# Three regroupings in a one-core block stack: the last projection by token blocks, narrow token sums in pairs, the recurrence's head norm half a round later

## The chip, the cores and the metric

The kernel runs on one core of one Trainium2 chip. The metric is the device time of one execution in microseconds (us). The kernel before was timed in three executions: 1313.74, 1315.18 and 1315.96 us, so the median is 1315.18 us. One more execution was taken with the hardware profiler; its own time is 1314.39 us, and the span that its page covers is 1312.6 us.

Five engines work side by side: PE (TensorE, matrix products into PSUM banks of 128 x 512 fp32), DVE (VectorE), ACT (ScalarE), POOL (GpSimd) and SP (SyncE, which here only issues DMAs).

## What is computed

Everything is for one sequence of 512 tokens and a model width of 1024. Two blocks run one after the other. The first has a gated MLP layer and a chunked attention layer and ends in a norm. The second takes that norm's output `x`, and has two branches:

```python
h = rms_norm(x, norm_g)
hq, hf, hi, hz, cq, ckv, kr, mz, gl = split(h @ w_in)
# branch 1: a gated linear recurrence over 8 heads of 128, then a norm per head
o = hgrn2_recurrence(silu(hq), 1 - f, hi, log(f))       # f from sigmoid(hf)
o = rms_norm_2(o, hg_norm_g) * silu(hz)                 # mean over the 128 channels of a head
# branch 2: latent attention over 8 heads -> out2 * silu(mz)
y = sigmoid(gate0) * (o @ w_proj_a) + sigmoid(gate1) * (out2 @ w_proj_b)
x = x + y @ w_out                                        # the last projection, 1024 x 1024
return rms_norm(x, final_norm_g)                         # per token, over 1024 features
```

`rms_norm` multiplies by `rsqrt(mean(x*x) + 1e-6)` and by a gain per feature. The change touches three places of this: the norm of `h` at the start of the second block (its sums over features), the norm of `o` per head, and the last projection with the residual and the final norm behind it.

## The kernel before, in words

**Layout.** Activations lie with features on the 128 partitions and the 512 tokens along the free axis: `x` is 8 tiles of 128 x 512. A product of fp32 accuracy is three products in the rounded type fp32r, high x high, low x high and high x low (`mm3`, lines 497 to 502). PE takes an fp32r product of 128 x 512 as one instruction; a plain fp32 product shows as two in the trace.

**Weights.** They come from HBM as slabs of 128 x 1024 fp32 in the order of the list `ORDER`. For each slab SP issues a DMA into one of two `raw` buffers (L474), ACT rounds it into `whi` (`cut`, L1075), POOL subtracts to get `wlo` (L490), and PE waits for that. `whi` and `wlo` have four places each, so `cut` waits until PE has used the slab four earlier. The last projection has 8 slabs (`w3`); the first four of them are put into a part of `yhi`/`ylo` that is free by then, and are loaded between the slabs of the second branch's projection (`pb`).

**A slab of PE work** is `slab(...)`: 8 blocks k, three products each, 24 in all. Its argument `between` lets other small work in behind a block k.

**The second block's first norm.** The values projection (`values(0)`, slabs `hv`) starts before the norm's factors are known. When two of its four slabs are done, `token_factors` (L743 to L749) sums the squares of every token: 8 products of one column each, plain fp32, four with `nacc` and four with `naccb`. DVE and ACT turn these into one factor per token, DVE writes them as diagonal matrices (`diag`, L1818), PE spreads them over all partitions by one plain fp32 product of 128 x 512 with a matrix of ones (L741), and DVE multiplies (`nfull`, L1825), ACT and DVE round (`hhi`, `hlo`, L1829). The next slab, `hq` of head 0, waits for `hlo` block by block.

**The recurrence.** Round r projects head r (slabs `hq`, `hf`, `hz`, and `mz` for the other branch) and runs head s = r - 1 through scores, state updates and outputs in between. The norm of head u = r - 2 is: ACT squares the output (`ho`, L1296), PE sums over the 128 channels by a plain fp32 product of 128 x 512 with ones (`hg_square`, L787, behind block 2 of slab `hq`), ACT takes Ln and Exp (L1298, L1300), DVE multiplies and rounds (`hg_finish`: L1854, L1857, L1859, L1861). On ACT `hg_root(u)` stands at the start of a round, on DVE `hg_finish(u)` too. The chain of a round that others hang on goes from the end of slab `hf` over ACT's Sigmoid and Ln (L1339, L1340) and a DVE scan to the rounded queries and keys (last of them `hqxlo`, L1935), which PE needs for `hg_diagonal` behind block 4 of the next `hq`.

**The end.** With `pb` PE alternates slabs of the second gate (`g1`). `x` had been kept in HBM and is loaded back; PE spreads the first block's norm factors by an fp32 product (L996) and DVE applies them (`normed`, L2079). The last projection runs in 16 steps of 24 products of 128 x 256 (`out_slab`): features on the partitions, tokens in two halves. DVE adds each result to `x` (L2106), ACT squares (L1513), DVE accumulates. For each half PE sums over the partitions (`out_tokens`, L1025, L1026: eight narrow products), DVE and ACT work out the factors, PE spreads them (`out_wide`, L1031) and DVE multiplies (`finished`, L2129); SP stores each 128 x 256 tile (L478). For the second half all this comes behind the last product.

## Time and profile before

| what | value |
|---|---|
| median of three executions | 1315.18 us (1313.74 to 1315.96) |
| profiled execution's own time | 1314.39 us |
| its span | 1312.6 us, 16685 instructions |
| PE busy | 1295.1 us (99%), 6531 instructions |
| DVE busy | 729.9 us (56%) |
| ACT busy | 664.4 us (51%) |
| POOL busy | 496.0 us (38%) |
| granted clock of PE | 0.996 of full speed over the span |
| HBM read, written | 123.92 MB, 10.49 MB |

The page gives for each engine the time in which it had an instruction under way. A product's end is modelled and products overlap, so what a product costs is read from the distance between two starts, not from its own duration: rows of 0.39 us for 128 x 512 follow each other every 0.23 us. A bracket at a row's end is the time in which the engine had nothing to do before it, and what ended that. Some records of products are missing from the trace.

### The profile page before, as it was taken

The page shows a single profiled execution, that of the slowest core. Times are in us where ns is not written, and L with a number is a line of the kernel's source. Part 1 is how long each engine was busy: PE and PEld are TensorE (multiplying, and loading weights), DVE is VectorE, ACT ScalarE, POOL GpSimd, SP SyncE. Part 2 cuts the span into 40 slices and gives each one's busy share as a digit, 9 for nine tenths or more (in the row PEclk, how much of TensorE's full clock was granted, in tenths as well). Part 3 has the DMA queues.
Part 4 walks back from the last instruction along what each step waited for, and adds up shares of the span by engine and source line. Part 5 has one row for each costly group of instructions (what it writes and reads, how often), then busy time and mean ns, then how long its engine had stood idle before and what let it go on. Part 6 is the DMA issues. An engine that isn't in the chain of part 4 may idle for free.

```text
span 1312.6 us, 16685 instructions
## 1 busy us (share of the span) xinstructions
PE 1295.1 (99%) x6531; PEld 1087.0 (83%) x6531; DVE 729.9 (56%) x1305; ACT 664.4 (51%) x999; POOL 496.0 (38%) x207
## 2 busy tenths in 40 slices
PE   9999999999999999999999999999999999999997
PEld 7888888888887788888878888888878888888897
DVE  5556556561146465555875577666645556643554
ACT  5535544443234666675546566666445545552321
POOL 4443444434444323221536343333333333334620
PEclk9999999999999999999999999999999999999999
DMA  5732322334333322322343322222223222335411
GB/s 183 262 118 90 103 84 86 100 94 150 98 112 95 96 80 94 96 63 64 95 148 111 93 65 80 70 77 65 80 81 99 78 80 82 90 105 174 154 41 65
DMA packets 43455, 131.31 MB, mean 100 GB/s; under 512 B 7088, under 2 KB 11888, under 8 KB 42864
## 3 DMA queue, kind: packets, MB, share of 16 engines
q1 hardware_dynamic: 38144, 116.41, 28.9%
q10 hardware_dynamic: 5232, 13.83, 3.0%
q8 instruction: 52, 0.85, 0.3%
q14 instruction: 27, 0.22, 0.1%
HBM read 123.92 MB, written 10.49 MB: 102 GB/s over the span
## 4 chain that ended last, share of the span: by engine, by line
PE 80%; DVE 11%; ACT 6%; issue 2%; POOL 0%; DMA 0%; DVEq 0%; SPq 0%; ACTq 0%
PE banks L500 24%; PE banks L502 24%; PE banks L501 24%; PE banks L681 2%; DVE hd L1897 1%; PE banks L673 1%; PE banks L662 1%; DVE naccb L1802 1%; DVE ylo L1699 1%; PE banks L596 1%; ACT L1340 1%; ACT L1339 1%; PE banks L906 1%; PE banks L787 1%; DVE hb L1894 1%
## 5 line engine op out<-in xcount | busy, mean ns | idle before, releaser
L490 POOL TENSOR_TENSOR wlo<-raw,whi 128x1024 fp32r<-128x1024 f32 (+2 forms) x198 | 485.0, 2452 | 738.4 <-ACT whi L1075 738.2
L500 PE MATMUL banks<-hhi,whi 128*128 128x512 f32 x752 | 304.5, 405 | 2.2 <-DVE hlo L1829 1.2
L502 PE MATMUL banks<-hlo,whi 128*128 128x512 f32 x752 | 294.1, 391 | 0.0
L501 PE MATMUL banks<-hhi,wlo 128*128 128x512 f32 x752 | 294.0, 391 | 0.0
L1075 ACT ACTIVATE whi<-raw 128x1024 fp32r<-128x1024 f32 (+2 forms) x198 | 205.4, 1038 | 170.9 <-PE banks L502 104.5
L500 PE MATMUL banks<-yhi,whi 128*128 128x512 f32 x448 | 176.8, 395 | 0.2 <-DVE ylo L1699 0.2
L502 PE MATMUL banks<-ylo,whi 128*128 128x512 f32 x448 | 174.7, 390 | 0.0
L501 PE MATMUL banks<-yhi,wlo 128*128 128x512 f32 x448 | 174.5, 389 | 0.0
L500 PEld LDWEIGHTS banks<-hhi,whi 128*128 128x128 f32 x752 | 141.9, 189 | 32.1 <-issue 2.9
L502 PEld LDWEIGHTS banks<-hlo,whi 128*128 128x128 f32 x752 | 141.5, 188 | 30.4
L501 PEld LDWEIGHTS banks<-hhi,wlo 128*128 128x128 f32 x752 | 142.1, 189 | 26.9 <-issue 2.2
L500 PEld LDWEIGHTS banks<-yhi,whi 128*128 128x128 f32 x448 | 84.1, 188 | 21.0 <-issue 3.2
L502 PEld LDWEIGHTS banks<-ylo,whi 128*128 128x128 f32 x448 | 84.1, 188 | 18.0
L501 PEld LDWEIGHTS banks<-yhi,wlo 128*128 128x128 f32 x448 | 84.2, 188 | 17.3 <-issue 0.2
L500 PE MATMUL banks<-whi,yhi 128*128 128x512 f32 x224 | 88.6, 396 | 0.7 <-DVE ylo L1555 0.6
L502 PE MATMUL banks<-wlo,yhi 128*128 128x512 f32 x224 | 87.2, 389 | 0.0
L501 PE MATMUL banks<-whi,ylo 128*128 128x512 f32 x224 | 87.2, 389 | 0.0
L500 PEld LDWEIGHTS banks<-whi,yhi 128*128 128x128 f32 x224 | 42.0, 188 | 11.4 <-issue 1.2
L501 PEld LDWEIGHTS banks<-whi,ylo 128*128 128x128 f32 x224 | 42.1, 188 | 8.9 <-issue 0.5
L502 PEld LDWEIGHTS banks<-wlo,yhi 128*128 128x128 f32 x224 | 42.0, 188 | 8.7
L1212 ACT ACTIVATE sc<-sc,sm 128x128 f32<-128x128 f32 (+1 forms) x64 | 35.1, 550 | 27.5 <-DVE sm L1757 27.5
L1655 DVE TENSOR_TENSOR mt<-mt,sz 128x512 f32<-128x512 f32 x16 | 26.3, 1642 | 37.8 <-ACT sz L1155 37.5
(383 smaller groups left out, 2205.9 us busy)
## 6 DMA issues: line engine op xcount, KB each, us to landing
raw<-w SPq DMA_DIRECT2D x193, 512.0 KB, 3.6
rel_tab<-relx ACTq DMA_DIRECT2D x1, 4096.0 KB, 21.0
tab<-rel_tab SPq DMA_DIRECT2D x16, 224.0 KB, 3.5
x<-xt ACTq DMA_DIRECT2D x1, 2048.0 KB, 9.3
x_kept<-x ACTq DMA_DIRECT2D x1, 2048.0 KB, 7.5
parts_kept<-mcg SPq DMA_DIRECT2D x8, 256.0 KB, 4.4
mgt<-parts_kept SPq DMA_DIRECT2D x8, 256.0 KB, 4.0
x<-x_kept ACTq DMA_DIRECT2D x1, 2048.0 KB, 8.0
```

The costliest lines, as they stand in the source:

```text
L490: nc.gpsimd.tensor_tensor(lo[:, begin:width], raw[:, n % 2, begin:width], f32(hi[:, begin:width]), ALU.subtract).then_inc(lo_done, 1)
L500: nc.tensor.matmul(dst, a[0], b[0], start=first, stop=False)
L501: nc.tensor.matmul(dst, a[1], b[0], start=False, stop=False)
L502: return nc.tensor.matmul(dst, a[0], b[1], start=False, stop=last)
L596: nc.tensor.matmul(mixes[q][:, t, :, :], vhi[:, t, cols], wts[:, q, :, :], start=True, stop=False)
L662: done = nc.tensor.matmul(banks[:, c:c + QW[t]], a[rows, t * P:(t + 1) * P], b[rows, 0:QW[t]], start=first, stop=last)
L673: last = nc.tensor.transpose(banks[:, c:c + P], sc[:, q, of:of + P], ident)
L681: last = nc.tensor.matmul(bank[AO[i][q]][:, k * P:S], av[q][:, i, k, :], p[:, q, AK[q][k]:AK[q][k] + KW[k]], start=k == 0 and p is phi, st ...
L787: nc.tensor.matmul(bank[6], ones, ho[:, 0, :], start=True, stop=True).then_inc(hoP.did("ms"), 1)
L1075: nc.scalar.activation(parts(slab)[0][:, begin:width], raw[:, n % 2, begin:width], ACT.Copy).then_inc(hi_done, 1)
L1212: e = nc.scalar.activation(row, row, ACT.Exp, bias=sm[:, q, 1, t:t + 1], accum_out=sm[:, q, 2, t:t + 1])
L1655: V.tensor_tensor(mt[:, q, :], mt[:, q, :], sz[:, q, :], ALU.mult).then_inc(uzV.did(f"y{q}"), 1)
```

## The change

**1. Token sums in pairs.** The eight narrow products no longer stand in one block between the second and third slab of `values(0)`. Each pair (one of `nacc`, one of `naccb`) follows one group of the third slab: behind blocks t = 1, 2, 3 of k = 4 and t = 0 of k = 5. The spreading product moves from behind the third slab to behind k = 6, t = 0 in the fourth.

**2. The head's norm half a round later.** ACT rounds the square into `hsqhi` and DVE the rest into `hsqlo`, both fp32r. PE sums them by two fp32r products with ones (`hones`), now behind block 1 of slab `hf` instead of block 2 of `hq`. ACT's Ln and Exp move from the round's start to behind the query's Silu; DVE's `hg_finish` moves behind the third state and ahead of `hstlo`. The sum goes to bank 2 (bank 6 for the last head), so slab `hz` waits for the Ln that reads it.

**3. The last projection by token blocks.** The product is turned: 8 groups (g, t), g a half of the features and t one of four token blocks, each with `mgh`/`mgl` stationary and four slabs' columns moving, 24 products of 128 x 512. Each group has a PSUM bank of its own. For that the residual `x` is turned too: PE transposes it in 32 products of 128 x 128 (`residual_turned`, half of them behind `pb` 2, half behind `pb` 4), and `normed` reads them with a token's factor as a scalar per partition and the gain from `fin1`, a row of 1024 spread over the partitions by DMA. ACT squares each result and sums along the free axis in the same instruction; the final factor is then a number per partition, with no product on PE. DVE finishes the upper feature half, ACT the lower, and each stores its own (SP and ACT queue, 128 x 512 each). The last four `w3` slabs come in another order, so that they lie in the ring's places in order.

```diff
-    return order + [("w3", n) for n in range(KT)]
+    return order + [("w3", n) for n in (0, 1, 2, 3, 6, 7, 4, 5)]
...
+W3B = (2, 3, 4, 5, 6, 7, 0, 1)
+GROUPS = [(g, t) for g in range(2) for t in range(TT)]
...
@@ PE, values(half) @@
-                    if half == 0 and j == 2:
-                        token_factors()
...
                             done = mm3(bank[4 + t], a, b, k == 0, k == KT - 1)
+                            if half == 0 and 1 <= TT * (k - 4) + t <= TT:
+                                token_sums(TT * (k - 4) + t - 1)
+                            if half == 0 and k == KT - 2 and t == 0:
+                                pe.wait_ge(n2V.sem, n2V.at("diag"))
+                                nc.tensor.matmul(bank[3], ones, diag[:, 0, :], start=True,
+                                                 stop=True).then_inc(n2P.did("wide"), 1)
...
@@ PE, the recurrence @@
             def hg_square(u):
-                pe.wait_ge(hoA.sem, hoA.at("sq", u))
-                pe.wait_ge(htV.sem, htV.at("far", u))
-                nc.tensor.matmul(bank[6], ones, ho[:, 0, :], start=True, stop=True).then_inc(hoP.did("ms"), 1)
+                pe.wait_ge(hoV.sem, hoV.at("sqlo", u))
+                if u < HH - 1:
+                    pe.wait_ge(htA.sem, htA.at("z", u + 1))
+                else:
+                    pe.wait_ge(htV.sem, htV.at("far", u))
+                nc.tensor.matmul(sum_bank(u), hones[:, :], hsqhi[:, :], start=True, stop=False)
+                nc.tensor.matmul(sum_bank(u), hones[:, :], hsqlo[:, :], start=False, stop=True).then_inc(hoP.did("ms"), 1)
 
             def hg_scores(r, k):
                 s, u = r - 1, r - 2
-                if k == 2 and u >= 0:
-                    hg_square(u)
...
             def hg_updates(s, k):
+                if k == 1 and s >= 1:
+                    hg_square(s - 1)
...
+                if r >= 2:
+                    pe.wait_ge(hoA.sem, hoA.at("ln", r - 2))
                 slab("hz", r, bank[2], h, between=outputs)
...
@@ PE, the end @@
+            def residual_turned(g):
+                if g == 0:
+                    pe.wait_ge(ld_x3, 16)
+                    pe.wait_ge(mtV.sem, mtV.all())
+                else:
+                    pe.wait_ge(x3V.sem, x3V.at(f"x{TT - 1}"))
+                for t in range(TT):
+                    for k in range(TT):
+                        last = nc.tensor.transpose(bank[4 + t][:, k * P:(k + 1) * P], x[:, TT * g + k, t * P:(t + 1) * P], ident)
+                last.then_inc(x3P.did(f"turn{g}"), 1)
...
+            def out_group(at, ks=range(KT)):
+                g, t = GROUPS[at]
+                pe.wait_ge(lo_done, max(LD["w3", TT * g + c] for c in range(TT)) + 1)
+                rows = slice(t * P, (t + 1) * P)
                 for k in ks:
                     if at == 0:
                         pe.wait_ge(mgV.sem, mgV.at("lo", k))
+                    last = mm3(bank[W3B[at]], (mgh[:, k, rows], mgl[:, k, rows]),
+                               [u[:, :, k * P:(k + 1) * P] for u in w3_parts[g]], k == 0, k == KT - 1)
+                if KT - 1 in ks:
+                    last.then_inc(w3P.did(f"g{at}"), 1)
...
@@ ACT @@
+            def hg_square(u):
                 if u >= 1:
                     act.wait_ge(hoV.sem, hoV.at("ylo", u - 1))
                 act.wait_ge(htP.sem, htP.at("o", u))
                 nc.scalar.activation(ho[:, 0, :], bank[3], ACT.Square).then_inc(hoA.did("sq"), 1)
+                act.wait_ge(hoA.sem, hoA.at("sq", u))
+                act.wait_ge(hpV.sem, hpV.at("k", min(u + 1, HH - 1)))
+                nc.scalar.activation(hsqhi[:, :], ho[:, 0, :], ACT.Copy).then_inc(hoA.did("sqhi"), 1)
+
+            def hg_root(u):
                 act.wait_ge(hoP.sem, hoP.at("ms", u))
...
                     hg_query(r)
+                    if u >= 0:
+                        hg_root(u)
                     cut()
                     hg_forget(r)
...
             act.dma_start(x[:, :, :], xs).then_inc(ld_x3, 16)
+            act.dma_start(fin1[:, :], fins[0, :].partition_broadcast(P)).then_inc(ld_fin, 16)
+            act.dma_start(fin2[:, :], fins[1, :].partition_broadcast(P)).then_inc(ld_fin, 16)
...
+            for at, (g, t) in enumerate(GROUPS):
+                if at < 2:
+                    cut()
+                    cut()
+                act.wait_ge(w3V.sem, w3V.at(f"x{at}"))
+                nc.scalar.activation(mgt[:, at % 2, :], x[:, at, :], ACT.Square,
+                                     accum_out=rt3[:, 0, g, t:t + 1]).then_inc(w3A.did(f"sq{at}"), 1)
+                if g == 1:
+                    act.wait_ge(w3V.sem, w3V.at(f"inv{t}"))
+                    nc.scalar.activation(rt1[:, 2, t:t + 1], rt1[:, 1, t:t + 1], ACT.Sqrt).then_inc(w3A.did(f"root{t}"), 1)
+                    act.wait_ge(w3A.sem, w3A.at(f"root{t}"))
+                    nc.scalar.activation(x[:, t, :], x[:, t, :], ACT.Copy,
+                                         scale=rt1[:, 2, t:t + 1]).then_inc(w3A.did(f"low{t}"), 1)
+                    act.wait_ge(w3A.sem, w3A.at(f"low{t}"))
+                    act.dma_start(out[t, :, 0:S], x[:, t, :]).then_inc(st_out, 16)
...
@@ DVE @@
+            def hg_square(u):
+                dve.wait_ge(hoA.sem, hoA.at("sqhi", u))
+                V.tensor_tensor(hsqlo[:, :], ho[:, 0, :], f32(hsqhi[:, :]), ALU.subtract).then_inc(hoV.did("sqlo"), 1)
...
+                if s >= 1:
+                    hg_finish(s - 1)
                 dve.wait_ge(htA.sem, htA.at("sthi", s))
                 V.tensor_tensor(hsts[1][:, :, :], hst[:, :, :], f32(hsts[0][:, :, :]),
                                 ALU.subtract).then_inc(htV.did("stlo"), 1)
...
                 if r >= 2:
-                    hg_finish(r - 2)
+                    hg_square(r - 2)
...
+            for at, (g, t) in enumerate(GROUPS):
+                dve.wait_ge(w3P.sem, w3P.at(f"g{at}"))
+                V.tensor_tensor(x[:, at, :], x[:, at, :], bank[W3B[at]], ALU.add).then_inc(w3V.did(f"x{at}"), 1)
+                if 1 <= at <= TT:
+                    gained(at - 1)
+                if at == TT:
+                    V.tensor_scalar(rt3[:, 1, 0, :], rt3[:, 0, 0, :], 1.0 / D, EPS, ALU.mult, ALU.add).then_inc(w3V.did("part"), 1)
+                    dve.wait_ge(w3V.sem, w3V.at("part"))
+                if g == 1:
+                    one = slice(t, t + 1)
+                    dve.wait_ge(w3A.sem, w3A.at(f"sq{at}"))
+                    V.scalar_tensor_tensor(rt1[:, 0, one], rt3[:, 0, 1, one], 1.0 / D, rt3[:, 1, 0, one], ALU.mult,
+                                           ALU.add).then_inc(w3V.did(f"mean{t}"), 1)
+                    dve.wait_ge(w3V.sem, w3V.at(f"mean{t}"))
+                    V.reciprocal(rt1[:, 1, one], rt1[:, 0, one]).then_inc(w3V.did(f"inv{t}"), 1)
+                    dve.wait_ge(w3A.sem, w3A.at(f"root{t}"))
+                    V.scalar_tensor_tensor(x[:, at, :], x[:, at, :], rt1[:, 2, one], fin2[:, S:D], ALU.mult,
+                                           ALU.mult).then_inc(w3V.did(f"high{t}"), 1)
```

How the instructions stand now, at three places. Line numbers of the changed kernel are its own.

PE in a middle round of the recurrence, before: the fp32 sum (L787) stands behind block 2 of slab `hq`, ahead of the key transposes (L758).

```order
L500 MATMUL banks<-hhi,whi 128x512
L501 MATMUL banks<-hhi,wlo 128x512
L502 MATMUL banks<-hlo,whi 128x512
L787 MATMUL banks<-ho,cst 128x512
L500 MATMUL banks<-hhi,whi 128x512
L501 MATMUL banks<-hhi,wlo 128x512
L502 MATMUL banks<-hlo,whi 128x512
L758 MATMUL banks<-cst,hkb 128x128 x3
```

After: two fp32r products (`hsqhi`, `hsqlo` with `hones`) behind block 1 of slab `hf`.

```order
L505 MATMUL banks<-hhi,whi 128x512
L506 MATMUL banks<-hhi,wlo 128x512
L507 MATMUL banks<-hlo,whi 128x512
L796 MATMUL banks<-hsqhi,hones 128x512
L797 MATMUL banks<-hsqlo,hones 128x512
L505 MATMUL banks<-hhi,whi 128x512
L506 MATMUL banks<-hhi,wlo 128x512
L507 MATMUL banks<-hlo,whi 128x512
```

The one instruction of plain fp32 is gone from `hq`, and two rounded ones stand a slab later, ahead of the state updates.

ACT in the same round, before: from the rounding of the scores (L1323) over the query's Silu (L1333) and a slab's rounding (L1075) to Sigmoid and Ln (L1339, L1342) and the rounding of the states (L1327).

```order
L1323 ACTIVATE hshi<-hs 128x512
L1333 ACTIVATE hq<-banks 128x512
L1075 ACTIVATE whi<-raw 128x1024
L1339 ACT_TABLE_LOAD
L1339 ACTIVATE he<-banks 128x512
L1340 ACT_TABLE_LOAD
L1342 ACTIVATE hf<-he,lb 128x512
L1327 ACTIVATE hsthi<-hst 128x384
L1075 ACTIVATE whi<-raw 128x1024
```

After: Ln and Exp of the norm (L1298, L1300) stand between the Silu and the slab's rounding (L1070 now), each with a table load of its own.

```order
L1323 ACTIVATE hshi<-hs 128x512
L1333 ACTIVATE hq<-banks 128x512
L1298 ACT_TABLE_LOAD
L1298 ACTIVATE ho<-banks,cst 128x512
L1300 ACT_TABLE_LOAD
L1300 ACTIVATE ho<-ho 128x512
L1070 ACTIVATE whi<-raw 128x1024
L1339 ACT_TABLE_LOAD
L1339 ACTIVATE he<-banks 128x512
L1340 ACT_TABLE_LOAD
L1342 ACTIVATE hf<-he,lb 128x512
L1327 ACTIVATE hsthi<-hst 128x384
```

Two activations moved in here and brought two table loads, where there were none with them before.

DVE at the very end, before: the last residual sum (L2106), the second half's factors (L2121 to L2125), and eight tiles to finish (L2129).

```order
L2106 TENSOR_TENSOR x<-x,banks 128x256
L2121 TENSOR_SCALAR rt<-banks 128x2
L2123 RECIPROCAL rt<-rt 128x2
L2125 TENSOR_TENSOR nr<-cst,rt 128x256
L2129 SCALAR_TENSOR_TENSOR x<-x,vec,banks 128x256 x8
```

After: the last residual sum (L2118), one token block's factor (L2127, L2130), one tile to finish (L2132), behind the finishing of the block before.

```order
L2130 RECIPROCAL rt<-rt 128x1
L2132 SCALAR_TENSOR_TENSOR x<-x,rt,fin 128x512
L2118 TENSOR_TENSOR x<-x,banks 128x512
L2127 SCALAR_TENSOR_TENSOR rt<-rt 128x1
L2130 RECIPROCAL rt<-rt 128x1
L2132 SCALAR_TENSOR_TENSOR x<-x,rt,fin 128x512
```

Of the eight finishing multiplications of 128 x 256 behind the last product, one of 128 x 512 is left on DVE (one of the same size is now ACT's), and the diagonal matrix that PE had to spread is gone.

## Rows read from the trace of the kernel before

**Rows 1.** Timeline of PE, one recurrence round: start, duration, engine, line, operation, tiles.

```profile
870.04 0.39 PE L502 MATMUL banks<-hlo,whi 128*128 128x512 f32 x1
870.58 1.12 PE L787 MATMUL banks<-ho,cst 128*128 128x512 f32 x2 [0.15 <-ACT ho L1296]
...
871.78 0.40 PE L501 MATMUL banks<-hhi,wlo 128*128 128x512 f32 x1
...
873.28 0.22 PE L500 MATMUL banks<-hqxhi,hkhi 128*128 128x128 f32 x1
```

**Rows 2.** Timeline of ACT, middle of the same round.

```profile
851.46 0.58 ACT L1333 ACTIVATE hq<-banks 128x512 f32<-128x512 f32 x1
855.17 1.06 ACT L1075 ACTIVATE whi<-raw 128x1024 fp32r<-128x1024 f32 x1 [3.13 <-PE banks L502]
856.25 1.28 ACT L1339 ACT_TABLE_LOAD   x1
```

**Rows 3.** Timeline of ACT, the norm of the last head.

```profile
963.62 0.69 ACT L1298 ACTIVATE ho<-banks,cst 128x512 f32<-128x512 f32 x1 [4.42 <-PE banks L787]
...
965.62 0.63 ACT L1300 ACTIVATE ho<-ho 128x512 f32<-128x512 f32 x1
```

**Rows 4.** Timeline of DVE, the round of rows 1 and 2.

```profile
845.02 2.50 DVE L1859 CAST yhi<-ho 128x512 fp32r<-128x512 f32 x1
...
860.72 0.56 DVE L1886 TENSOR_TENSOR hstlo<-hst,hsthi 128x384 fp32r<-128x384 f32 x1 [5.97 <-ACT hsthi L1327]
...
870.60 1.09 DVE L1935 TENSOR_TENSOR hqxlo<-hqx,hqxhi 128x896 fp32r<-128x896 f32 x1
```

**Rows 5.** Timeline of PE, the token sums in the values projection.

```profile
667.40 1.02 PE L747 MATMUL banks<-cst,nacc 128*128 128x1 f32 x8 [0.34 <-DVE naccb L1802]
...
669.49 0.40 PE L501 MATMUL banks<-whi,ylo 128*128 128x512 f32 x1
...
684.58 0.50 PE L500 MATMUL banks<-hhi,whi 128*128 128x512 f32 x1 [0.64 <-DVE hlo L1829]
```

**Rows 6.** Timeline of DVE, the factors written as diagonals.

```profile
670.81 0.69 DVE L1818 TENSOR_TENSOR diag<-cst,rt 128x512 f32<-128x512 f32 x1 [0.27 <-ACT rt L1282]
```

**Rows 7.** Timeline of PE, ten transposes of 128 x 128 in the attention.

```profile
1040.83 1.25 PE L906 MATMUL banks<-cst,msc 128*128 128x128 f32 x10
...
1042.15 0.40 PE L501 MATMUL banks<-hhi,wlo 128*128 128x512 f32 x1
```

**Rows 8.** Timeline of PE, the slab behind the fourth slab of `pb`.

```profile
1222.50 0.47 PE L500 MATMUL banks<-hhi,whi 128*128 128x512 f32 x1 [0.31 <-POOL wlo L490]
```

**Rows 9.** Timeline of PE: last `pb` slab, last projection's first and last product.

```profile
1249.78 0.39 PE L500 MATMUL banks<-yhi,whi 128*128 128x512 f32 x1
...
1255.22 0.28 PE L500 MATMUL banks<-mgh,yhi 128*128 128x256 f32 x1
...
1302.31 0.28 PE L502 MATMUL banks<-mgl,whi 128*128 128x256 f32 x1
```

**Rows 10.** Line 590, moving operand in two strided runs: ns min/median/max, starts.

```profile
L590 PE MATMUL banks<-wts,rones x16: 282/282/386, 113.9 to 275.9; 128*128 128x256 f32 x16
```

**Rows 11.** Timeline of DVE, behind the last product.

```profile
1302.62 0.42 DVE L2106 TENSOR_TENSOR x<-x,banks 128x256 f32<-128x256 f32 x1 [0.73 <-PE banks L502]
1304.70 0.16 DVE L2121 TENSOR_SCALAR rt<-banks 128x2 f32<-128x2 f32 x1 [1.66 <-PE banks L1026]
...
1305.33 0.42 DVE L2125 TENSOR_TENSOR nr<-cst,rt 128x256 f32<-128x256 f32 x1 [0.27 <-ACT rt L1517]
1306.55 3.22 DVE L2129 SCALAR_TENSOR_TENSOR x<-x,vec,banks 128x256 f32<-128x256 f32 x8 [0.79 <-PE banks L1031]
```

**Rows 12.** Timeline of ACT: what an accumulating activation adds.

```profile
1172.72 0.19 ACT L1488 ACTIVATION_READ_ACCUMULATOR msc<-msc,msm 128x1 f32 x1
```

**Rows 13.** DMA issues: tiles, queue, count, size of one, us to landing.

```profile
raw<-w SPq DMA_DIRECT2D x193, 512.0 KB, 3.6
...
out<-x SPq DMA_DIRECT2D x16, 128.0 KB, 1.8
```

234 lines of the change are left out of this document (76 added, 158 removed).

## The prediction, made before the changed kernel was run

> **What bounds the kernel now.** I read the page's table of busy times first: PE has something under way in 99% of the span, no other engine in more than 56%. So a microsecond of PE's work or of PE's waiting is a microsecond of the kernel, work on DVE, ACT or POOL counts only where PE waits for it, and DMA only at the very end. Then I read PE's own timeline at the places that the diff touches. Distances between starts are the price list. A 128 x 512 product in fp32r takes 0.227 us: the last `pb` slab has 24 of them in 5.44 us [rows 9]. The reader is to see four things. In a recurrence round PE first waits for ACT's square and then spends long on the plain fp32 sum [rows 1]. In the values projection it waits for DVE and then does narrow sums [rows 5]. The last projection takes from 1255.22 to 1302.31 us [rows 9]. Behind its last product 10.3 us pass until the span's end at 1312.6, with DVE doing eight multiplications at the end of them [rows 11].
>
> **Part 2, the head's norm.** From 870.04 to 871.78 there are 1.74 us in which two ordinary distances (0.45) would stand, so wait and fp32 sum together cost 1.29: 0.31 of wait (0.54 between the first two starts, less 0.23) and 0.97 for the sum (870.58 to 871.78, less 0.23) [rows 1]. Two fp32r products cost 0.45. Seven heads stand in this position, one every 29.6 us, all with the same distances: 7 x (1.29 - 0.45) = 5.9 us. The last head's sum has no wait before it: 0.97 - 0.45 = 0.5. Together -6.3 to -6.4; I take **-6.3**.
>
> That counts the wait as gone, so what is late next? On the clock of before: PE's first diagonal product stood at 873.28 [rows 1], and without the 1.29 us it stands at 872.0. It needs `hqxlo`, ready at 870.60 + 1.09 = 871.69 [rows 4]. 0.3 us are left, less the hand-off. I take that as no wait; if it fails it costs what is missing, seven times.
>
> In the round's middle Ln and Exp are inserted on ACT with a table load each, ahead of the slab rounding at 855.17, which starts when slab `hf` ends, and the Sigmoid behind it, from which the round's chain starts [rows 2]. The slab now holds the sum, so it ends 0.45 later, at 855.6. If the query's Silu ends where it did, at 851.46 + 0.58 = 852.04, the insert ends at 852.04 + 1.28 + 0.69 + 1.28 + 0.63 = 855.9 [rows 2, 3], 0.3 late. But the Silu stands behind a rounding that waits for DVE's masks, and DVE's masks stood behind `hg_finish`, with a cast that alone takes 2.50 [rows 4]; with that moved away I estimate the Silu 0.7 earlier and the insert's end at 855.2. So the cover is ACT's idle 3.13 us before 855.17 [rows 2], and I take nothing for it. Between the two ends, 0 and 0.3 us a round, lies up to 2 us.
>
> The new waits: `hg_square` on PE waits for DVE's rest of the square (`hsqlo`), made more than half a round before; queued behind it is all of slab `hf`. Slab `hz` waits for the Ln, which ends near 853.9 at the latest, when `hf` is not yet through. On DVE `hg_finish` now starts near 855.3 and takes the cast's 2.50 and three operations of 128 x 512 at about 0.7 each (estimated from 1.09 for 128 x 896 [rows 4]), 4.6 in all, to 859.9. Behind it is `hstlo`, which waits for ACT until 860.72, and 0.45 later now [rows 4]. It is in time by over 1 us, in the 5.97 us that DVE stood idle. The rounding of the square and the earlier slab rounding on ACT fall where nobody waits.
>
> **Part 1, the pairs.** The block of sums runs from 667.40 to 669.26 (669.49 less 0.23), after a wait of 0.34 [rows 5]: 1.86 us for eight. Pairs between long products I price the same, 0.45 each. PE saves the wait, since the first pair comes 1.4 us later than the block did. But it is not PE that this stage ends with: slab `hq` waits for `hlo` at 684.58 and PE stands for 0.64 us there [rows 5], and that chain starts at the spreading product. Before, that came 24 products behind the sums: 669.26 + 5.44 = 674.7. Now it comes behind nine groups of three (6.1 us) and four pairs (1.8 us), counted from 667.06: 675.0. The factors are ready: they took until 670.81 + 0.69 = 671.50 [rows 6], 2.24 behind the sums, and the last pair now ends at 667.06 + 3.4 + 1.8 = 672.3, which gives 674.5. So what PE saves it gives back as a longer wait for `hlo`: **+0.2**, between -0.5 (wait gone, nothing given back) and +0.5.
>
> **Part 3, the stage with `pb`.** Off goes one fp32 spreading product: -0.97, by the sum in [rows 1]. On come 32 transposes of 128 x 128; ten take 1042.15 - 0.23 - 1040.83 = 1.09 us [rows 7], so 32 take +3.5. POOL's late slab costs PE 0.31 at 1222.50, about 0.4 with the restart [rows 8]; PE will now come there 0.97 earlier and 1.75 (sixteen transposes) later, 0.8 late in sum, while POOL's slabs hang on loads and not on PE. That wait goes: -0.4. Sum **+2.1**. The gains `fin1` and `fin2` put 1 MB more on the DMA engines. At 3.6 us for 512 KB [rows 13] that is up to 7 us of transfer. It is issued right behind the load of `x`, when all four places of the ring are full, and is needed some 25 us later, so I take 0 of a possible 0 to 3.
>
> **The last projection.** Before: 1255.22 to 1302.31 + 0.12 = 47.2 us, with 384 products, one set of token sums and one spreading product inside [rows 9]. After: 192 x 0.227 = 43.5. **-3.7.** The moving operand now lies in four runs of 128. Were each run to cost like a product of its own, 0.11 [rows 7], it would be 4 x 0.11 - 0.23 = 0.21 more per product, 40 us in all. Line 590 streams 256 columns in two such runs in 282 ns [rows 10], the same as the 0.28 of a contiguous 256 [rows 9], so I take nothing.
>
> **Behind the last product.** Before: 10.3 us from its start. After, from the start of the last one: DVE begins 0.42 later (0.31 for 256 columns [rows 11], 0.11 more of streaming), adds 512 columns (0.73 with the hand-off), ACT squares (0.63 as the Exp [rows 3]) and reads the accumulator (0.19 [rows 12]), mean, reciprocal and root take 1305.33 - 1304.70 = 0.63 [rows 11], and DVE's last multiplication 0.75, while ACT does its half beside it. That is 3.4. Then two stores of 256 KB. One of 128 KB lands in 1.8, a load of 512 KB in 3.6 [rows 13]; I take 3.0, since both run together, and 0.1 for hand-offs. 6.5 against 10.3: **-3.8**, with ends -5.0 and -3.2.
>
> **Sum.** -6.3 + 0.2 + 2.1 - 3.7 - 3.8 = -11.5 us. From the profiled execution's own 1314.4 that gives 1302.9; the median of the three runs stands 0.8 above that execution, which would give 1303.7. I forecast 1303.3.
>
> **Rivals.**
> A, slower. The insert on ACT is not covered. It decides from the point where Exp ends more than 0.3 us behind the end of `hf`: from there the Sigmoid, the scan and `hqxlo` come late by the same amount, PE waits at the diagonal, and every microsecond counts seven times. It turns the forecast into a loss from 1.9 us of lateness. If a table load held the engine as long again as its 1.28, the insert would end at 857.8, 2.2 behind 855.6: 7 x 1.9 = 13.3, and the time is 1314.4 - 11.5 + 13.3 = 1316.2. Against it: between Ln's end at 964.31 and Exp's start at 965.62 there are 1.31 us, just one load [rows 3]. For it: three loads in a row is a pattern with no idle time between them that the trace does not show. The Trainium skill, page "ScalarE: Activation LUTs", section "What ACT_TABLE_LOAD costs", states a load of about 1283 ns and a drain of about 1380 ns on top for each change of set. By that rule two more changes a round would come to 2.8 us more than I count, and as an estimate the time would be near 1317; the trace has the load at that length and no drain beside it, so the trace decides. 5%.
> B. The chain takes over in the rounds. The 0.3 us of room at the diagonal products is used up by hand-offs and by ACT's insert, and PE waits 0.3 to 0.4 there each round: 7 x 0.35 = 2.5 less gain, 1305.8. The narrow room speaks for it; DVE's lighter start of a round speaks against. 15%.
> C. The end gives less: the two final stores are slow (3.6 or more instead of 3.0), or the 1 MB delays a slab while `pb` runs and PE waits 2 us more. 1305.8. The wait at 1222.50 [rows 8] shows that slabs are tight there. 13%.
> D. The stage does not do what it says: a strided moving operand streams slower than rows 10 shows for two runs. Even a tenth of the bound above is 4 us: 1307. 3%.
> The forecast itself has 64%, with its own range from 1301 to 1305.
>
> **How the numbers follow.** A measurement of this kernel tells no change from about 0.2% (2.6 us). A, 5%, is slower, or close to no change if milder. B, C and D are faster, as the forecast is; two of them together still are. I set faster 0.92, same 0.03, slower 0.05. The range takes in the low ends (-0.5 in part 1, -5.0 at the end: 1301) and B and C together at the high end: 1300.5 to 1308.
>
> **What would show it.** Right: no product of `ho` in PE's timeline, `hsqhi` and `hsqlo` 0.23 apart, and round period 28.8 instead of 29.6; ACT's slab rounding in the middle still begins when PE ends `hf`; transposes in two blocks of 1.75 us; groups of 5.44 us; the span ends 6 to 7 us behind the last product. Wrong: ACT goes from Exp straight into the rounding with PE's `hf` long done; a wait of PE for `hqxlo`; a wait for POOL between `pb` 2 and `pb` 5; products of 128 x 512 in the last projection more than 0.24 apart.

## The result

The changed kernel takes 1306.56 us (median of five executions, 1304.92 to 1310.23), the one before 1315.18. The ratio is 0.9934, with a 95% interval of 0.9924 to 0.9944: 8.6 us by the medians. The two profiled executions differ by 9.5 us (1314.39 and 1304.92; spans 1312.6 and 1303.1). The forecast was 1303.3 with a range of 1300.5 to 1308, so the time lies inside, 3.3 us above the point.

Busy times first, from the page of the kernel after:

```profile
span 1303.1 us, 16288 instructions
...
PE 1286.9 (99%) x6349; PEld 1077.0 (83%) x6349; DVE 728.6 (56%) x1286; ACT 690.1 (53%) x1027; POOL 498.4 (38%) x207
```

PE still bounds everything. Its busy time has fallen by 8.2 us. The other 1.3 us are a balance of idle time: behind the last product PE stands 2.2 us less, in the middle rounds 1.0 less, in the last round 1.6 more.

The two timelines of PE can be laid side by side, since the same products stand in both. What the starts of the same product differ by, after less before, at the marks between the stages (the last column is the step from one mark to the next):

| mark (a product of PE) | before | after | step |
|---|---|---|---|
| first product with `hkb`, end of the first norm's stage | 724.07 | 724.28 | +0.21 |
| first product with `hkthi`, last round | 940.03 | 934.77 | -5.47 |
| first product with `hqbhi`, last round | 952.58 | 949.08 | +1.76 |
| sums of `dsq`, downward projection | 975.77 | 971.93 | -0.34 |
| spreading of `ddiag` | 984.77 | 979.57 | -1.36 |
| last product with `msc`, end of attention | 1174.49 | 1169.40 | +0.11 |
| first product of the last projection | 1255.22 | 1252.26 | +2.13 |
| last product of the last projection | 1302.31 | 1296.65 | -2.70 |
| end of the span | 1312.6 | 1303.1 | -3.84 |

The sum is -9.5.

**The middle rounds went as forecast.** PE's timeline after, in the sixth round; it answers to [rows 1]. Columns: start and duration in us, engine, line, result and operands, shape, count.

```profile
868.04 0.49 PE L765 MATMUL banks<-cst,hkb 128*128 128x128 f32 x3
...
869.07 0.22 PE L505 MATMUL banks<-hqxhi,hkhi 128*128 128x128 f32 x1
...
875.23 0.39 PE L796 MATMUL banks<-hsqhi,hones 128*128 128x512 f32 x1
875.46 0.39 PE L797 MATMUL banks<-hsqlo,hones 128*128 128x512 f32 x1
875.69 0.39 PE L505 MATMUL banks<-hhi,whi 128*128 128x512 f32 x1
```

The two rounded products cost 0.23 each, and no row carries a bracket: no wait for the square, none for `hqxlo` at the diagonal products (869.07). ACT's timeline of the same kernel one round earlier, to be held against [rows 2, 3]; the bracket at the end is idle time before the instruction and what ended it:

```profile
847.16 0.58 ACT L1333 ACTIVATE hq<-banks 128x512 f32<-128x512 f32 x1
847.76 1.28 ACT L1298 ACT_TABLE_LOAD   x1
849.06 0.69 ACT L1298 ACTIVATE ho<-banks,cst 128x512 f32<-128x512 f32 x1
849.76 1.28 ACT L1300 ACT_TABLE_LOAD   x1
851.06 0.63 ACT L1300 ACTIVATE ho<-ho 128x512 f32<-128x512 f32 x1
852.26 1.06 ACT L1070 ACTIVATE whi<-raw 128x1024 fp32r<-128x1024 f32 x1 [0.56 <-PE banks L507]
```

The insert ends at 851.69, and the slab rounding still waits 0.56 us for PE: it is covered, with that much room. The period of a round is 28.85 us (before 29.62).

**The last round did not.** The same insert there, on ACT, DVE, POOL and PE:

```profile
938.80 1.06 ACT L1070 ACTIVATE whi<-raw 128x1024 fp32r<-128x1024 f32 x1 [5.00 <-PE banks L507]
939.87 1.28 ACT L1298 ACT_TABLE_LOAD   x1
941.17 0.69 ACT L1298 ACTIVATE ho<-banks,cst 128x512 f32<-128x512 f32 x1
...
943.83 0.75 DVE L1863 SCALAR_TENSOR_TENSOR ho<-banks,vec,ho 128x512 f32<-128x512 f32 x1 [5.46 <-ACT ho L1300]
...
945.38 2.63 POOL L495 TENSOR_TENSOR wlo<-raw,whi 128x1024 fp32r<-128x1024 f32 x1 [3.04 <-ACT whi L1070]
945.80 2.75 DVE L1870 TENSOR_TENSOR ylo<-ho,yhi 128x512 fp32r<-128x512 f32 x1
948.48 0.55 DVE L1897 TENSOR_TENSOR hstlo<-hst,hsthi 128x384 fp32r<-128x384 f32 x1
949.08 0.33 PE L505 MATMUL banks<-hqbhi,hsthi 128*128 128x128 f32 x1 [1.59 <-DVE hstlo L1897]
```

PE waits 1.59 us for `hstlo`. Two things stand in its way. ACT idles 5.00 us at a slab rounding that stands ahead of Ln, so DVE's finish of head 6 starts only at 943.83. And DVE's `ylo`, 0.69 us where nothing else runs, takes 2.75 beside POOL's slab.

**The end.** PE's blocks of transposes and the last projection, and DVE's and ACT's work behind the last product; they answer to [rows 7, 9, 11, 12]:

```profile
1205.17 1.91 PE L1010 MATMUL banks<-cst,x 128*128 128x128 f32 x16
...
1228.71 1.91 PE L1010 MATMUL banks<-cst,x 128*128 128x128 f32 x16
...
1252.26 0.40 PE L505 MATMUL banks<-yhi,mgh 128*128 128x512 f32 x1
...
1296.65 0.40 PE L507 MATMUL banks<-wlo,mgh 128*128 128x512 f32 x1
1297.08 0.69 DVE L2118 TENSOR_TENSOR x<-x,banks 128x512 f32<-128x512 f32 x1 [2.73 <-PE banks L507]
...
1299.19 0.75 DVE L2132 SCALAR_TENSOR_TENSOR x<-x,rt,fin 128x512 f32<-128x512 f32 x1 [0.27 <-ACT rt L1524]
```

From 1252.26 to 1296.65 there are 191 distances of 0.2324 us, not 0.227. Behind the last product 3.3 us of work and 3.1 us of store follow, 6.45 in all.

**A stretch of half clock** in the profiled run of before makes the step of -1.36 at `ddiag`. Windows at the same place of the program, three of before and then one of after (the window ahead of it has 1.00 as well); the column ahead of the last two is PE's granted clock:

```profile
972.00:976.00 4.00, 2.71 (x13) 1.93 (x13) 3.90 (x4) 1.25 (x2) 2.60 (x1) 1.00 0.45 133
976.00:980.00 4.00, 4.00 (x24) 3.53 (x24) 3.81 (x7) 0.34 (x2) 2.37 (x1) 0.86 0.45 141
980.00:984.00 4.00, 4.00 (x14) 3.17 (x13) 2.30 (x5) 3.95 (x5) 0.86 (x1) 0.71 0.16 56
```

```profile
972.00:976.00 4.00, 4.00 (x26) 3.62 (x27) 3.84 (x6) 0.40 (x1) 2.37 (x1) 1.00 0.49 139
```

In both PE has just waited 1.3 us for DVE's sums of `dsq`. Before, the clock then fell from 2.4 to 1.2 GHz for a while: 0.14 x 4 + 0.29 x 4 = 1.7 us lost. After, it did not, in that execution. In others it seems to: the kernel after has mean clocks of 0.995 to 0.999, and its execution of 0.995 is the slow one, 1310.23. Between the marks the stretch cost less than 1.7, namely the 1.36 of the table. So 1.4 of the 9.5 us between the two profiled executions is chance, and the medians' 8.6 is the fairer number.

### The profile page after: what moved, and what is told of

Read it like the earlier page. It is cut to its first block, busy times and chain, and to the rows that moved or that the text cites. A ratio compares the mean times of both kernels' runs of the same rounds, so it can differ in the third digit from the quotient of the medians.

```text
span 1303.1 us, 16288 instructions
## 1 busy us (share of the span) xinstructions
PE 1286.9 (99%) x6349; PEld 1077.0 (83%) x6349; DVE 728.6 (56%) x1286; ACT 690.1 (53%) x1027; POOL 498.4 (38%) x207
## 4 chain that ended last, share of the span: by engine, by line
PE 92%; DVE 5%; ACT 2%; issue 1%; DMA 0%; SPq 0%; DVEq 0%; ACTq 0%
PE banks L505 28%; PE banks L507 28%; PE banks L506 28%; PE banks L686 2%; PE banks L678 1%; PE banks L667 1%; DVE ylo L1702 1%; PE banks L601 1%; PE banks L919 1%; DVE nfull L1698 1%; DVE hlo L1832 0%; DVE nfull L1828 0%; DMA raw<-w 0%; PE banks L951 0%; PE banks L950 0%
## 5 line engine op out<-in xcount | busy, mean ns | idle before, releaser
L505 PE MATMUL banks<-hhi,whi 128*128 128x512 f32 x752 | 300.3, 399 | 2.5 <-DVE hlo L1832 1.9
L1070 ACT ACTIVATE whi<-raw 128x1024 fp32r<-128x1024 f32 (+2 forms) x198 | 205.3, 1038 | 155.7 <-PE banks L507 98.2
```

The source lines that it names most:

```text
L505: nc.tensor.matmul(dst, a[0], b[0], start=first, stop=False)
L1070: nc.scalar.activation(parts(slab)[0][:, begin:width], raw[:, n % 2, begin:width], ACT.Copy).then_inc(hi_done, 1)
```

## The experiments

In each the marks above were read again. The front part of the program starts up to 0.7 us later or earlier from one execution to the next, so distances between marks are compared, and times of whole executions only with their ratio.

### The head's norm alone

The kernel before, with only this part of the change (its main lines, against the kernel before):

```diff
@@ PE, hg_updates @@
+                if k == 1 and s >= 1:
+                    hg_square(s - 1)
...
@@ ACT @@
                     hg_query(r)
+                    if u >= 0:
+                        hg_root(u)
...
@@ DVE, hg_stage @@
+                if s >= 1:
+                    hg_finish(s - 1)
```

> The kernel before with only the head's norm changed (two rounded products behind block 1 of slab hf, Ln and Exp in the round's middle). Theory: the terms are separate and add. Seven rounds get 0.78 us shorter each (-5.5), the last head's sum gives -0.3, and in the last round PE waits for hstlo, +1.8, because DVE does the whole finish of head 6 ahead of it. Sum -4.0: about 1311.2 by median, round period 28.85 us, one wait of PE of 1.6 us near 949 us + 0 in the last round. Rival: the wait for hstlo comes only with the other parts of the change (other phase of POOL and DVE); then the sum is -5.8, 1309.4, and PE has no wait for hstlo.

1311.16 us (ten executions, 1309.74 to 1313.99), ratio to before 0.9967 (0.9958 to 0.9976). The last round's `hkthi` stands at 934.59, 5.44 us earlier than before; then comes:

```profile
948.90 0.33 PE L508 MATMUL banks<-hqbhi,hsthi 128*128 128x128 f32 x1 [1.59 <-DVE hstlo L1917]
```

The wait for `hstlo` belongs to this part and to no other. The rival is out. The -4.0 us expected was measured as -4.0 at the sums of `dsq` (971.75 against 975.77), and as -4.6 by the medians.

### Contiguous moving operand

```diff
-                               [u[:, :, k * P:(k + 1) * P] for u in w3_parts[g]], k == 0, k == KT - 1)
+                               [u[:, k // 2, (k % 2) * S:(k % 2 + 1) * S] for u in w3_parts[g]], k == 0, k == KT - 1)
...
-            "pb": _feature_slabs(i["w_proj_b_2"][0]), "w3": _feature_slabs(i["w_out_2"][0])}
+            "pb": _feature_slabs(i["w_proj_b_2"][0]), "w3": _token_slabs(i["w_out_2"][0])}
```

> The changed kernel, but the last projection's weights lie in the slabs by pairs of blocks k, so that the moving operand of each product is 512 contiguous columns instead of four runs of 128. Nothing else is different. Theory: the runs cost. Distance between products in the last projection falls from 0.2324 to 0.2267 us, 192 x 0.0057 = 1.1 us, first to last product 43.3 us, and the kernel is 1.1 us faster than the changed one (about 1305.5). Rival: the longer distance comes from something else in that stretch (the stationary operand, DVE and ACT in the same memory, the banks); then the distance stays 0.232 and the time is that of the changed kernel (1306.6).

The theory fell. From first to last product it is 1298.08 - 1253.68 = 44.40 us, as in the changed kernel (44.39). Four runs of 128 cost nothing. The time, 1308.13 us (six executions, 1305.10 to 1310.38), is no different from the changed kernel's within their spreads.

### The last round's Ln and Exp first

```diff
                 else:
-                    cut()
                     hg_root(u)
                     hg_states(s)
                     cut()
+                    cut()
```

> The changed kernel, but in the last round ACT does head 6's Ln and Exp and the rounding of the states ahead of the slab rounding for which it waits 5 us. Theory: PE's wait of 1.6 us for hstlo (at 949.08 us) is caused by Ln and Exp standing behind that slab rounding; with them at about 934 instead of 940 us DVE has finished head 6 by about 942 and hstlo is there by 943, 4 us ahead of PE. The wait and its restart go: -1.8 us, about 1304.8 by median. Rival 1: ACT's slab rounding then comes late and PE waits for a slab instead, gain 0 to 0.5. Rival 2: what PE saves it gives back at the downward projection's wait of 1.3 us (970 to 972 us), which then grows to 3 us; gain 0.

1304.86 us (1304.70 to 1306.58), ratio 0.9922 (0.9910 to 0.9934). DVE's timeline:

```profile
938.82 0.75 DVE L1863 SCALAR_TENSOR_TENSOR ho<-banks,vec,ho 128x512 f32<-128x512 f32 x1
...
940.79 2.77 DVE L1870 TENSOR_TENSOR ylo<-ho,yhi 128x512 fp32r<-128x512 f32 x1
943.49 0.55 DVE L1897 TENSOR_TENSOR hstlo<-hst,hsthi 128x384 fp32r<-128x384 f32 x1
```

The finish starts 5 us earlier, `hstlo` is there at 944.04, and PE's wait is gone. From `hkthi` to the sums of `dsq` it is 35.34 us instead of 37.16: -1.82, as expected, with the wait at `dsq` unchanged at 1.30. No slab came late there; PE waited 0.39 us once for POOL in the `pb` stage.

### The narrow sums in a block, the spreading product earlier

```diff
-                            if half == 0 and 1 <= TT * (k - 4) + t <= TT:
-                                token_sums(TT * (k - 4) + t - 1)
-                            if half == 0 and k == KT - 2 and t == 0:
+                            if half == 0 and k == 4 and t == 1:
+                                for tt in range(TT):
+                                    token_sums(tt)
+                            if half == 0 and k == 5 and t == 1:
```

> The changed kernel, but all eight narrow sums stand in one block where the first pair stands (behind block t = 1 of k = 4), and the spreading product stands 12 products later (behind t = 1 of k = 5). Theory: what ends this stage is the chain spreading product, nfull, hlo, not PE. The block costs PE what four pairs cost (0 to 0.1 us difference), the spreading product starts near 672.7 us instead of 674.9, and PE's three waits for hlo (1.31, 0.28 and 0.30 us) go: -1.5 to -2.0 us, about 1304.8 by median. Rival 1: pairs between long products are cheaper than a block; then the block costs more (+0.5 or more) and the gain is 1.0 to 1.4. Rival 2: hlo is late because DVE and ACT, not the spreading product, are behind; the waits stay, gain 0. In both, PE may wait for the diagonal at the new place if the factors take over 2.5 us.

1304.96 us (1303.33 to 1308.10), ratio 0.9924 (0.9912 to 0.9936). Changed kernel first, then the experiment:

```profile
674.94 1.02 PE L743 MATMUL banks<-diag,cst 128*128 128x512 f32 x2
...
684.78 0.50 PE L505 MATMUL banks<-hhi,whi 128*128 128x512 f32 x1 [1.31 <-DVE hlo L1832]
...
686.03 0.50 PE L505 MATMUL banks<-hhi,whi 128*128 128x512 f32 x1 [0.28 <-DVE hlo L1832]
```

```profile
673.25 1.02 PE L744 MATMUL banks<-diag,cst 128*128 128x512 f32 x2
...
685.63 0.50 PE L505 MATMUL banks<-hhi,whi 128*128 128x512 f32 x1 [0.30 <-DVE hlo L1833]
```

From the first sums with `naccb` to the first product with `hkb` it is 53.74 us instead of 55.81: -2.07. The stage ends with the chain that starts at the spreading product. In a block or in pairs, the sums cost PE the same (1.79 and 1.81 us); what counts is where the spreading product stands.

One link of that chain is longer than it need be. In the changed kernel, DVE and POOL ahead of PE's wait of 1.31 us:

```profile
681.76 2.41 POOL L495 TENSOR_TENSOR wlo<-raw,whi 128x1024 fp32r<-128x1024 f32 x1 [4.66 <-ACT whi L1070]
682.50 2.22 DVE L1832 TENSOR_TENSOR hlo<-nfull,hhi 128x512 fp32r<-128x512 f32 x1
```

The other `hlo` take 0.69 us. This one takes 2.22 and ends 0.55 us behind POOL's slab; at 0.69 it would have ended at 683.19, ahead of PE's own arrival near 683.3. The experiment leaves that stretch in place (2.25 us) and only brings it forward, out of PE's way. No run moved POOL's slab here.

### One table load instead of two

```diff
             def hg_root(u):
+                act.preload_act_table_set("natural_log_exp_and_others")
                 act.wait_ge(hoP.sem, hoP.at("ms", u))
```

> The changed kernel, but ahead of Ln the set of ACT's tables is loaded that has both Ln and Exp, so that one load of 1.28 us stands in the insert instead of two. Theory: the insert ends 0.56 us ahead of the slab rounding that waits for PE (852.26 us), so it is covered, and a shorter one brings nothing: round period stays 28.85 us, the rounding's idle time grows from 0.56 to 1.84 us, time 1306 (as the changed kernel, within 1 us). In the last round Exp ends 1.3 us earlier, with it hstlo, and PE's wait there shrinks from 1.6 to 0.3 us: -1.3 us once. Rival: the insert is part of the round's chain; then each of six rounds gets up to 0.4 us shorter, -2.5 us more.

1303.41 us (1302.53 to 1304.45), ratio 0.9908 (0.9891 to 0.9924). The rounds keep their period of 28.85 us: the insert was covered, and the rival is out. But the last part gains more than the expected 1.3: from `hkthi` to the sums of `dsq` it is 34.08 us instead of 37.16. The wait for `hstlo` goes completely (-1.8) and not only by 1.3: DVE reaches `ylo` at 945.02, ahead of POOL's slab at 945.87, and `ylo` takes 0.69 us instead of 2.75. The wait at `dsq` goes too (-1.3), because the last head's Ln and Exp also stand on the way to DVE's sums of `dsq`. That second place the expectation had missed.

### One load more

```diff
                 nc.scalar.activation(ho[:, 1, :], ho[:, 1, :], ACT.Exp, scale=-0.5).then_inc(hoA.did("root"), 1)
+                for n in range(1):
+                    act.preload_act_table_set(("natural_log_exp_and_others", "exp_and_others")[n % 2])
```

> The changed kernel with one more load of a table (1.28 us) behind Exp in every head's insert. Theory: the insert has 0.56 us of room until the slab rounding, and hqxlo behind it 0.28 us until PE's diagonal products (ready at 868.77, wanted at 869.05). So 1.28 us more makes PE wait 0.44 us for hqxlo in each of the six middle rounds, +2.6 us, and another 1.3 us in the last round (hstlo later): about 1310.5, round period 29.3. Rival 1 (the forecast's rival A taken as a rule: every microsecond of ACT's insert counts in full): +1.28 x 6 + 1.3 = +9.0, 1315.6. Rival 2 (more cover than counted): no wait at the diagonal, only the last round's +1.3: 1307.9.

1308.49 us (1307.31 to 1309.07), ratio 0.9943 (0.9928 to 0.9957). PE's wait, as expected within 0.1 us:

```profile
872.03 0.33 PE L505 MATMUL banks<-hqxhi,hkhi 128*128 128x128 f32 x1 [0.34 <-DVE hqxlo L1948]
```

Six rounds have it, and their period is 29.43 us: +0.58 each, of which 0.34 is wait and the rest restart and products that then stand further apart. ACT behind Exp:

```profile
853.52 0.63 ACT L1300 ACTIVATE ho<-ho 128x512 f32<-128x512 f32 x1
854.17 1.28 ACT L1302 ACT_TABLE_LOAD   x1
855.47 1.06 ACT L1070 ACTIVATE whi<-raw 128x1024 fp32r<-128x1024 f32 x1
```

So the forecast's rival A is real as a mechanism. The insert can grow by 0.56 + 0.28 = 0.84 us before PE waits: 0.56 until Exp ends with `hf`, and 0.28 of lateness behind that, where the forecast had said 0.3. The load occupies ACT for 1.28 us and the next instruction starts 0.02 behind it. The Trainium skill ("ScalarE: Activation LUTs", section "What ACT_TABLE_LOAD costs") adds a drain of some 1380 ns to each change of set; three loads close together show none here.

The last round, expected 1.3 us longer, was 1.8 us shorter. That is the most telling miss of the study:

```profile
948.09 1.28 ACT L1302 ACT_TABLE_LOAD   x1
...
949.82 1.05 ACT L1070 ACTIVATE whi<-raw 128x1024 fp32r<-128x1024 f32 x1
...
950.08 0.69 DVE L1872 TENSOR_TENSOR ylo<-ho,yhi 128x512 fp32r<-128x512 f32 x1
950.68 0.55 DVE L1899 TENSOR_TENSOR hstlo<-hst,hsthi 128x384 fp32r<-128x384 f32 x1
950.94 2.55 POOL L495 TENSOR_TENSOR wlo<-raw,whi 128x1024 fp32r<-128x1024 f32 x1 [4.34 <-ACT whi L1070]
```

DVE reaches `ylo` 11.04 us behind `hkthi`, in the changed kernel 11.03. Ln and Exp are no earlier. But the second slab rounding stands 1.3 us later on ACT, behind the added load, so POOL starts its slab only when `ylo` is through. `ylo` takes 0.69 instead of 2.75, and PE does not wait. With Ln, Exp and the slab rounding where the change put them, POOL's slab is what makes `hstlo` late. ACT's rounding runs beside `ylo` here and does not stretch it. In the changed kernel `ylo` ends 0.54 us behind POOL's end (948.55 and 948.01), as if nearly all of it had run only then. The Trainium skill says that ("SBUF — State Buffer", section "Who interferes with whom"): a DVE instruction with two inputs in the on-chip memory and a POOL instruction that reads from it need the same pair of ports, and the one that issues first holds it to its end. The trace agrees.

The third long wait of PE, 1.31 us at the sums of `dsq`, has the same shape in the changed kernel:

```profile
968.72 2.60 POOL L495 TENSOR_TENSOR wlo<-raw,whi 128x1024 fp32r<-128x1024 f32 x1 [0.98 <-ACT whi L1070]
969.00 2.87 DVE L2008 TENSOR_TENSOR dsq<-dsq 128x512 f32<-128x512 f32 x1
```

DVE's sum ends at 971.87, 0.55 us behind POOL's slab, and PE starts at 971.93. So all three waits of over a microsecond behind 680 us (for `hlo`, `hstlo` and `dsq`) end directly behind a DVE operation that POOL's slab has stretched, or behind the one after it. Only for `hstlo` did a run take the stretch away.

### Another stationary operand

This run and the next two were executed once each (1304.34, 1304.99 and 1306.69 us). They are read by the distances between products in their traces, not by their times.

```diff
-                    last = mm3(bank[W3B[at]], (mgh[:, k, rows], mgl[:, k, rows]),
+                    last = mm3(bank[W3B[at]], (hhi[:, k, rows], hlo[:, k, rows]),
```

> The changed kernel, but the last projection takes its stationary operand from hhi and hlo instead of mgh and mgl (so its result is another matrix; everything else stays). The run with 512 contiguous columns moving left the distance between products at 0.2324 us. Theory: the distance hangs on the tile that mgh and mgl are (where they lie or what they hold), since products of 128 x 512 with hhi, hlo, yhi, ylo and the weights stand 0.2267 to 0.228 us apart, and only those with lhi/llo in the latent projections and mgh/mgl here 0.233. Then the distance falls to 0.227 to 0.228 and the stretch from first to last product from 44.4 to 43.4 us. Rival: the distance belongs to the stage (moving weights, banks, what other engines do); it stays 0.232.

```profile
1252.76 0.39 PE L505 MATMUL banks<-yhi,hhi 128*128 128x512 f32 x1
...
1296.05 0.39 PE L507 MATMUL banks<-wlo,hhi 128*128 128x512 f32 x1
```

43.29 us, 0.2266 per product. The theory held: the missing 1.1 us hang on `mgh` and `mgl`.

### The same numbers at the old place

```diff
-                nc.scalar.activation(mgh[:, m, :], mcg[:, m % 2, :], ACT.Copy).then_inc(mhA.did("hi"), 1)
+                nc.scalar.activation(mgh[:, m, :], f32(hhi[:, m, :]), ACT.Copy).then_inc(mhA.did("hi"), 1)
```

and the same for `mgl` with `hlo`.

> The changed kernel, but ACT and DVE fill mgh and mgl with copies of hhi and hlo instead of the gated sum and its rest (so the result is another matrix). With hhi and hlo themselves as stationary operand the products stood 0.2267 us apart, with mgh and mgl 0.2324. Theory place: where the tile lies decides; the numbers are those of hhi and hlo now, and the distance stays 0.2324, first to last product 44.4 us. Theory contents: the numbers decide; the distance is 0.2267, 43.4 us.

```profile
1252.31 0.40 PE L505 MATMUL banks<-yhi,mgh 128*128 128x512 f32 x1
...
1296.71 0.40 PE L507 MATMUL banks<-wlo,mgh 128*128 128x512 f32 x1
```

44.40 us again. With the same contents as in `hhi` and `hlo` the distance is the long one, so it is the place and not the contents.

### The upper tiles shifted by 32 bytes

```diff
         g12 = sb("g12", [P, KT], F32)
+        sb("pad", [P, 8], F32)
```

> The changed kernel with one unused tile of 32 bytes per partition ahead of all tiles that share the upper part of the on-chip memory (mgh, mgl, lhi, llo and the recurrence's among them); nothing else is different. If the place decides by its offset within a short line, the last projection's products move from 0.2324 us to 0.2267, and those with lhi and llo from 0.233 too. If it is the region or the contents, they stay.

Nothing moved towards 0.227: 1298.42 - 1253.85 = 44.57 us, 0.2333 per product. So it is not the offset in a short line. `lhi` and `llo`, which lie in the same upper part of the memory, show the same long distance as moving operand in every kernel read (0.233 us, 0.234 in this run), while products that use only the tiles allocated ahead of them stand 0.227 apart. That the upper place makes the distance is the reading that fits all of these; where the border lies, and why, stays open, and no run placed `mgh` and `mgl` below it.

### The best version

The edits of "the narrow sums in a block", "the last round's Ln and Exp first" and "one table load" together.

> The changed kernel with three edits: the narrow sums in a block with the spreading product 12 products later, Ln and Exp ahead of the slab rounding in the last round, one table load instead of two in the insert. Theory: the first two gains add, since each takes away a wait at a place of its own: -1.7 and -1.8 us from undisturbed execution (1304.9), 1301.5; and with only one wait of over 1 us left there are fewer stretches of half clock behind waits, so the median lies within 2 us of the fastest run: 1302 to 1303. Rival: the downward projection's wait of 1.3 us (970 to 972 us) grows by what the last round saves; then 1303.3 to 1305.

1300.37 us (four executions, 1300.13 to 1301.30), ratio to before 0.9883 (0.9869 to 0.9898). The changed kernel has 0.9934 (0.9924 to 0.9944), so this is 0.5% faster still. It is also 1.6 us below the low end of what was expected: the wait at `dsq`, 1.3 us, went with the second table load and was not in the sum. Behind the first norm's stage PE has two waits left, one of 0.39 us at the end of attention and this one:

```profile
974.78 1.55 PE L966 MATMUL banks<-ddiag,cst 128*128 128x512 f32 x3 [0.32 <-DVE ddiag L2023]
```

The last product starts at 1291.84, 4.81 us ahead of the changed kernel's: 2.1 from the first place, 1.8 and 1.3 from the second and third, less 0.2 at that row and 0.15 at the start. All four executions lie within 1.2 us, the changed kernel's five within 5.3. The mean clocks are 0.998 or 0.999, where all the kernels with waits of 1.3 to 1.6 us behind 680 us that were executed more than once have 0.994 to 0.997 in some of theirs. Every stretch of half clock met in a trace before the program's end began within about 3 us behind such a wait, as in the run with the narrow sums in a block, of which one window follows (the wait for `hstlo` ends at 947.38; in the windows before and after it the clock is 1.00):

```profile
948.00:952.00 4.00, 4.00 (x15) 3.38 (x15) 0.00 (x0) 0.00 (x0) 0.00 (x0) 0.57 0.25 100
```

Such a wait is not always followed by one: the profiled executions of four kernels with such waits have none.

## Why the prediction was right, and where it was not

The time lies in the stated range, but outside the forecast's own 1301 to 1305, which had 64%. What took it in is the upper part of the range, put there for rivals B and C together, and neither came. So the range held for another reason than the one it was drawn for. The three misses below all point the same way, and none is hidden by another.

The forecast's mechanism held: PE's time was the kernel's time, and removing PE's work and waits in the rounds, the last projection's extra work and the tail gave what was left. Term by term, in the traces:

- **Part 2, -6.3 forecast.** The rounds gave -5.47 for seven, 0.78 each instead of 0.84, and the last head's sum -0.34 instead of -0.5. The margins that were said to be narrow were there: 0.28 us at the diagonal, and 0.56 us on ACT, where I had counted between 0.4 of room and 0.3 of lateness. The step that failed is the sentence that `hstlo` "is in time by over 1 us, in the 5.97 us that DVE stood idle". It was read in a middle round and taken for all. In the last round ACT's order is another, Ln stands behind a slab rounding that waits 5 us, and `hstlo` was 1.59 us late: +1.8. The part as a whole gave -4.0, not -6.3. The price of DVE's finish was right (4.6 us forecast, 943.83 to 948.55 measured), with the stretch by POOL on `ylo` in place of the cast's 2.50 in [rows 4]; without that stretch `hstlo` would have been in time even in the last round, as the run with one load more showed.
- **Part 1, +0.2.** Measured +0.2, and for the reason given: what PE saved came back as a longer wait for `hlo` (1.31 after 0.64). What the forecast did not see is that this wait owes its length to one `hlo` that takes 2.2 us beside POOL's slab, before and after.
- **Part 3 with `pb`, +2.1.** Measured +2.13. The two blocks of transposes cost 1.75 each, POOL's wait went, and the 1 MB of gains delayed nothing.
- **The last projection, -3.7.** Measured -2.70. The term was mis-sized: 0.2324 us per product, not 0.227, so groups of 5.58 us and not 5.44. The runs of the moving operand, which I had suspected and set to nothing, do cost nothing. The stationary operand's place costs 1.1 us, which I had not thought of.
- **Behind the last product, -3.8.** Measured -3.84; 3.3 us of work (forecast 3.4) and 3.1 of store (3.0 and 0.1).

The misses are 0.5 in the rounds and the last head's sum, 1.8 in the last round and 1.0 in the projection: -11.5 becomes -8.2, which is what the medians show (-8.6). The profiled pair shows -9.5, since before's execution carried a stretch of half clock and after's did not. Of the rivals none came. A would have needed an insert 0.84 us longer, B's wait at the diagonal did not occur, C's stores landed in 2.6 to 2.8 us (the page's medians), and D's strided operand is free; that the times of B and C (1305.8) and of D (1307) are near the measured one has nothing to do with their causes.

## What to carry to other kernels

Work that is moved in a loop has to be followed through the last pass as well: the order of the other engines is different there, and one wait in it took back a third of what seven passes had given. When an engine that prepares operands is late, look at what runs beside it before looking at its own order: an instruction of 0.7 us took 2.8 because of when another engine started, and delaying the other engine cured it. Each of the three long waits of TensorE behind 680 us ended behind such a stretched operation, though only one of them was tested. And the kernel without these waits had the narrowest spread, 1.2 us against 5.3; that is one kernel with four executions, so it is an observation and not yet a rule.

## What was not expected of the hardware

- Products of 128 x 512 in fp32r stand 0.2324 us apart when the stationary operand lies in `mgh` and `mgl`, and 0.2266 when it lies in `hhi` and `hlo`, with the same numbers in them.
- An added table load of 1.28 us made the last round shorter by 1.8 us.
- A DVE operation of 0.69 us took 2.2 to 2.9 when POOL's slab had started before it, and ended about 0.55 us behind POOL's end.
- 1.3 to 1.6 us of waiting on TensorE can be followed by a stretch at 1.2 GHz, which cost 1.0 to 1.6 us between the marks (3.0 in one execution). In the profiled executions it followed in seven of the eleven kernels that had such waits behind 680 us; behind a wait of 1.54 us near 435 us, which all kernels share, it followed in none.
